# Gated feed-forwards with both terms of a weight tile's upper half in one matmul of 512 columns

## The reference

```python
def conv_glu_ffn(h, w_in, conv_w, conv_b, w_out):
    """Up-projection -> causal depthwise conv (width 3) -> GeGLU -> down-projection."""
    S = h.shape[1]
    u = h @ w_in
    up = jnp.pad(u, ((0, 0), (CONV_WIDTH - 1, 0), (0, 0)))
    u = sum(conv_w[k] * up[:, k:k + S] for k in range(CONV_WIDTH)) + conv_b
    gate, val = jnp.split(u, 2, axis=-1)
    return (jax.nn.gelu(gate, approximate=True) * val) @ w_out
```

## Time and profile before

| | us |
|---|---|
| three runs | 904.54, 904.81, 908.03 (median 904.81) |
| the profiled execution's own time | 907.95 |
| its span, first to last instruction | 906.1 |
| PE busy with matmuls | 849.4 (94%) |
| DVE busy | 620.1 (68%) |
| ACT busy | 469.6 (52%) |
| POOL busy | 134.9 (15%) |
| mean granted TensorE clock | 0.985 of full speed |

### The profile page before, as it was taken

The page is one execution under the profiler, slowest core; times in us unless marked ns, Lnnn a source line. Parts: engine busy times, 40 slices in busy tenths (PEclk is TensorE's granted clock), DMA queues, the critical chain, the costliest instruction groups (busy, mean ns, idle before and its releaser), DMA issues.

```text
span 906.1 us, 15493 instructions
## 1 busy us (share of the span) xinstructions
PE 849.4 (94%) x6073; PEld 788.2 (87%) x6073; DVE 620.1 (68%) x815; ACT 469.6 (52%) x680; POOL 134.9 (15%) x131
## 2 busy tenths in 40 slices
PE   4997998998999999978999999999988799999997
PEld 4997887998899999968999999979776699999996
DVE  6876565669755555696776776877763767767776
ACT  5544667235444444455654554674664465545553
POOL 2261111005100000010112112000221011121110
PEclk9999999999999999999999999999999899999999
DMA  7962233462665555544355455435320444554541
GB/s 287 307 229 94 94 118 115 170 250 93 232 257 185 185 185 186 186 146 157 140 186 203 169 186 205 166 140 187 130 103 1 169 141 167 183 216 158 185 175 47
DMA packets 23064, 152.55 MB, mean 168 GB/s; under 512 B 2443, under 2 KB 3683, under 8 KB 5475
## 3 DMA queue, kind: packets, MB, share of 16 engines
q1 hardware_dynamic: 21648, 145.44, 45.1%
q10 hardware_dynamic: 1363, 6.37, 1.9%
HBM read 150.71 MB, written 1.09 MB: 168 GB/s over the span
## 4 chain that ended last, share of the span: by engine, by line
PE 67%; DVE 6%; ACT 2%; issue 1%; POOL 0%; DVEq 0%; POOLq 0%; ACTq 0%
PE up L974 13%; PE up L976 13%; PE up L975 13%; PE down L980 7%; PE down L981 6%; PE down L982 6%; DVE w_lo L1501 2%; PE up L1010 1%; PE down L1043 1%; PE down L1045 1%; PE down L1180 1%; PE down L1422 1%; PE down L1049 1%; PE up L1446 1%; DVE mid L1767 1%
## 5 line engine op out<-in xcount | busy, mean ns | idle before, releaser
L1501 DVE TENSOR_TENSOR w_lo<-w,w_hi 128x2048 fp32r<-128x2048 f32 x132 | 306.5, 2327 | 77.8 <-ACT w_hi L624 77.6
L974 PE MATMUL up<-x_lo,w_hi 128*128 128x256 f32 x1248 | 357.0, 286 | 1.3 <-DVE w_lo L1501 1.3
L975 PE MATMUL up<-x_hi,w_hi 128*128 128x256 f32 x1248 | 354.1, 284 | 0.0
L976 PE MATMUL up<-x_hi,w_lo 128*128 128x256 f32 x1248 | 354.1, 284 | 0.0
L624 ACT ACTIVATE w_hi<-w 128x2048 fp32r<-128x2048 f32 x132 | 251.6, 1908 | 71.1 <-PE down L982 27.5
L974 PEld LDWEIGHTS up<-x_lo,w_hi 128*128 128x128 f32 x1248 | 240.5, 193 | 3.7 <-DVE w_lo L1501 2.1
L975 PEld LDWEIGHTS up<-x_hi,w_hi 128*128 128x128 f32 x1248 | 240.6, 193 | 1.2
L976 PEld LDWEIGHTS up<-x_hi,w_lo 128*128 128x128 f32 x1248 | 240.4, 193 | 0.0
L980 PE MATMUL down<-w_hi,mid 128*128 128x512 f32 x256 | 100.1, 391 | 0.7 <-DVE w_lo L1501 0.7
L981 PE MATMUL down<-w_hi,mid 128*128 128x512 f32 x256 | 100.0, 391 | 0.0
L982 PE MATMUL down<-w_lo,mid 128*128 128x512 f32 x256 | 99.6, 389 | 0.0
(11 more groups left out here) (243 smaller groups left out, 1049.8 us busy)
## 6 DMA issues: line engine op xcount, KB each, us to landing
w<-w_stream SPq DMA_DIRECT2D x134, 1024.0 KB, 4.8
gates<-vec_store ACTq DMA_DIRECT2D x5, 1024.0 KB, 6.3
region<-rpb SPq DMA_DIRECT2D x2, 768.0 KB, 12.2
gates<-x_in SPq DMA_DIRECT2D x2, 512.0 KB, 4.1
result<-res SPq DMA_DIRECT2D x4, 256.0 KB, 2.0
con<-consts SPq DMA_DIRECT2D x1, 801.0 KB, 6.3
proj<-bands ACTq DMA_DIRECT2D x1, 544.0 KB, 5.2
gates<-vec_store ACTq DMA_DIRECT2D x1, 512.0 KB, 3.8
```

What stands on the lines that cost most here:

```text
L974: m(out_ap, w_hi[slot][:, w_cols:w_cols + P], xl, start=first, stop=False, skip_group_check=True)
L975: m(out_ap, w_hi[slot][:, w_cols:w_cols + P], xh, start=False, stop=False, skip_group_check=True)
L976: return m(out_ap, w_lo[slot][:, w_cols:w_cols + P], xh, start=False, stop=last, skip_group_check=True)
L1501: v.tensor_tensor(lo_of(n), w32[s][:, :], hi_of(n).bitcast(F32), ALU.subtract).then_inc(w_lo_ready, 1)
```

## The change

`x_hi` and `x_lo` become two halves of one tensor `x_both`, so that one matmul can stream both. The up units of the gated feed-forwards go through `glu_unit`: for each weight tile one matmul of `w_hi` with 512 columns (256 of `x_hi`, 256 of `x_lo`) and one of `w_lo` with 256 columns of `x_hi`, which is added to the half that holds the `x_lo` term. A weight tile now fills a whole bank of 512 columns, and a unit two banks. The four banks `up` and `aux` become one tensor `ups`; kind 0 always takes banks 2 and 3, kind 1 banks 0 and 1. Since `aux` is bank 1, the stage's second unit now waits for `rows_ready`. The first unit of a stage keeps its 48 matmuls of 256 columns but also writes the halves apart (`first_glu_unit`).

The two halves have to be added. ACT copies the upper halves of both banks to `probs[kind]` (a buffer that the attention uses elsewhere), 128 x 512; DVE adds them to the lower halves, waits for that result, and then multiplies with the row factors in place. `reads_before` now follows the kind and not the ring slot.

```diff
-        x_hi = [sb(f"x_hi{s}", [P, DC, T], F32R) for s in range(2)]
-        x_lo = [sb(f"x_lo{s}", [P, DC, T], F32R) for s in range(2)]
+        x_both = [sb(f"x_both{s}", [P, 2, DC, T], F32R) for s in range(2)]
+        x_hi = [x_both[s][:, 0, :, :] for s in range(2)]
+        x_lo = [x_both[s][:, 1, :, :] for s in range(2)]
...
-        up = [ctx.enter_context(nc.psum_tensor(f"up{b}", [P, 2 * T], F32)) for b in range(RING)]
-        aux = ctx.enter_context(nc.psum_tensor("aux", [P, 2 * T], F32))
+        ups = ctx.enter_context(nc.psum_tensor("ups", [P, RING + 1, 2 * T], F32))
+        up = [ups[:, b, :] for b in (0, 2, 3)]
+        aux = ups[:, 1, :]
...
+        def glu_bank(kind, t):
+
+            return ups[:, (2, 0)[kind] + t, :]
+
+        def glu_halves(kind):
+
+            both = ups[:, (2, 0)[kind]:(2, 0)[kind] + 2, :]
+            return both[:, :, 0:T], both[:, :, T:2 * T]
...
                 for kind in range(2):
+                    act.wait_ge(unit_done, at.unit(units[kind] + 1))
+                    a.activation(pair_view(probs[kind][:, :]), glu_halves(kind)[1], ACT.Copy).then_inc(low_copied, 1)
                     act.wait_ge(up_read, at.up(UP_INDEX[units[kind]] + 1))
...
+            def glu_unit(at, n, fill, kind):
+
+                s = n % RING
+                pe.wait_ge(w_lo_ready, at.unit(n + 1))
+                if reads_before(n):
+                    pe.wait_ge(up_read, at.up(reads_before(n)))
+                for t in range(2):
+                    bank = glu_bank(kind, t)
+                    for c in range(DC):
+                        w = slice(c * UC + t * P, c * UC + (t + 1) * P)
+                        m(bank, w_hi[s][:, w], x_both[fill % 2][:, :, c, :], start=(c == 0), stop=False,
+                          skip_group_check=True)
+                        ins = m(bank[:, T:2 * T], w_lo[s][:, w], x_hi[fill % 2][:, c, :], start=False, stop=(c == DC - 1),
+                                skip_group_check=True)
+                ins.then_inc(unit_done, 1)
...
-                first_unit(base, fill)
+                first_glu_unit(base, fill)
                 spread(k_pre)
-                unit(STRAIGHT, base + 1, fill)
+                pe.wait_ge(rows_ready, PRE.index(k_pre) + 1)
+                glu_unit(STRAIGHT, base + 1, fill, 1)
...
-                    dve.wait_ge(unit_done, at.unit(n + 1))
-                    v.tensor_tensor(glu_u[kind][:, :, 2:T + 2], pair_view(up[n % RING][:, :]),
+                    dve.wait_ge(low_copied, 2 * at.pair(first + j) + kind + 1)
+                    upper = glu_halves(kind)[0]
+                    chain.link(v.tensor_tensor(glu_u[kind][:, :, 2:T + 2], upper, pair_view(probs[kind][:, :]), ALU.add))
+                    v.tensor_tensor(glu_u[kind][:, :, 2:T + 2], glu_u[kind][:, :, 2:T + 2],
                                     twice(rows[k_pre % 2][:, 0:T]), ALU.mult).then_inc(up_read, 1)
```

More of the change, by code:

```diff
@@ L90, in glu_ups, with glu_kind @@
     return (base + 3 * j - 1, base + 3 * j) if j else (base, base + 1)
+def glu_kind(n):
+    for base in (U_GLU0, U_GLU1):
+        for j in range(PAIRS2):
+            if n in glu_ups(base, j):
+                return base, glu_ups(base, j).index(n)
+    return n % RING
 def output_tile_units():
@@ L106, in reads_before @@
 def reads_before(n):
-    return max([UP_INDEX[m] + 1 for m in UP_INDEX if m < n and m % RING == n % RING], default=0)
+    return max([UP_INDEX[m] + 1 for m in UP_INDEX if m < n and glu_kind(m) == glu_kind(n)], default=0)
 GATES_PAUSE = (1, 8)
@@ L401, in build @@
         conv_first = sem("conv_first")
+        low_copied = sem("low_copied")
         conv_ready = sem("conv_ready")
@@ L1026, in first_unit, with first_glu_unit, term @@
                         ins = term(lo_of(n), x_hi[fill % 2], c, False, True)
+                ins.then_inc(unit_done, 1)
[12 more added lines that the diff above has]
+                                skip_group_check=True)
+                ins.then_inc(unit_done, 1)
+            def first_glu_unit(n, fill):
+                low_last = n in far_hi
+                pe.wait_ge(*((w_hi_ready, n + 1) if low_last else (w_lo_ready, n + 1)))
+                if reads_before(n):
+                    pe.wait_ge(up_read, reads_before(n))
+                def term(w, x, c, half, first, last):
+                    for t in range(2):
+                        ins = m(glu_bank(0, t)[:, half * T:(half + 1) * T], w[:, c * UC + t * P:c * UC + (t + 1) * P],
+                                x[:, c, :], start=(first and c == 0), stop=(last and c == DC - 1), skip_group_check=True)
+                    return ins
+                for c in range(DC):
+                    pe.wait_ge(x_hi_ready, hi_ready(fill, c))
+                    term(hi_of(n), x_hi[fill % 2], c, 0, True, False)
+                    if not low_last:
+                        term(lo_of(n), x_hi[fill % 2], c, 0, False, True)
+                for c in range(DC):
+                    pe.wait_ge(x_ready, DC * fill + c + 1)
+                    ins = term(hi_of(n), x_lo[fill % 2], c, 1, False, True)
+                if low_last:
+                    pe.wait_ge(w_lo_ready, n + 1)
+                    for c in range(DC):
+                        ins = term(lo_of(n), x_hi[fill % 2], c, 0, False, True)
                 ins.then_inc(unit_done, 1)
@@ L1353, in glu @@
                 layer = (U_GLU0, U_GLU1).index(base)
-                first_unit(base, fill)
+                first_glu_unit(base, fill)
                 spread(k_pre)
-                unit(STRAIGHT, base + 1, fill)
+                pe.wait_ge(rows_ready, PRE.index(k_pre) + 1)
+                glu_unit(STRAIGHT, base + 1, fill, 1)
                 def units(at, j):
-                    unit(at, base + 3 * j - 1, fill)
-                    unit(at, base + 3 * j, fill)
+                    glu_unit(at, base + 3 * j - 1, fill, 0)
+                    glu_unit(at, base + 3 * j, fill, 1)
                     pe.wait_ge(mid_ready, PAIRS1 + PAIRS2 * layer + at.pair(j))
@@ L1370, in glu @@
                 for j in (PAIRS2 - 2, PAIRS2 - 1):
-                    for n in glu_ups(base, j):
-                        unit(STRAIGHT, n, fill)
+                    for kind, n in enumerate(glu_ups(base, j)):
+                        glu_unit(STRAIGHT, n, fill, kind)
                 made = PAIRS1 + PAIRS2 * (layer + 1)
@@ L1938, in glu @@
                     at = Looped(i, 4, 2)
-                    chain.enter(i, 4)
+                    chain.enter(i, 8)
                     glu_pair(at, base, layer, 3, k_pre)
```

## The result

The changed kernel took 930.14 us (median of 4 runs, 929.87 to 932.16), the kernel before 905.72 us beside it (median of 4, 904.54 to 908.03). The ratio is 1.0266 with a 95% interval of 1.0242 to 1.0291: slower, by about 24 us. The forecast was 931.1 us. Of all executions two were slow, one of experiment 3 (2199.19 us) and one of the kernel before beside experiments 5, 9 and 10 (1060.43 us); they are in no ratio and no interval, and without them those medians are 919.36 in place of 919.88 and 907.51 in place of 907.53.

What follows compares the result with a forecast made beforehand. PE was taken as the present bound (16.98 us a pair), a DVE-POOL-ACT chain as the new one (17.40). Start, body and tail summed to +14.0 and +12.3, together +26.3 on the median: 931.1 us, range 923 to 937.

Steps and rivals of the forecast that it cites:

- The closed chain: Loop pair: a cycle from DVE's first add through POOL and ACT's last split and copy back to it, 17.40 us.
- Multiply after 0.83: Loop pair, each kind: DVE's add to its multiply, 0.72 us plus 0.11 for the register-valued wait.
- The 0.11 for a wait whose value comes from a register: Extra cost of a DVE wait in the loop, read from taps of 1.90 us inside against 1.79 outside.
- the body: Each stage from pair 1 to pair 9: 138.3 us, +6.9 in layer 0 and +5.2 in layer 1.
- the forecast's rival of a cheaper add: DVE's add in the pairs costs less, without the register's 0.11 or at 0.60 us: 924.7 to 928.5 us; 15%.
- the 9.0 us: Merged matmuls in 42 up units: 0.0133 us per merge, 0.213 a unit, 9.0 us in all if PE stays the bound.
- the first rival: Loop: the new work fits and PE stays the bound, pair of 16.53 us or less, 906 us in all; 3%.
- The start: Each stage up to pair 1: PE's second unit waits for DVE's row-factor copy, +5.1 us per layer.
- 4.4 us of pause: Layer 0's start: PE's second unit waits from 420.14 to the end of DVE's row-factor copy at 424.55.
- a loss of 1.7: Both starts: PE at 1.2 GHz for 3.4 us behind the pause, 1.7 us lost each, bounds 0 and 3.4.
- The tail: Each stage from pair 9 to its end: 35.6 us for 33.6, +2.0 a layer; 26.2 to the last mid_lo.
- the rival of more frequent falls: The clock falls also after PE's pauses in pairs 1 and 10, 1.7 us each, up to four: up to 938; 10%.

Runs made afterwards that it cites:

- experiment 3: Changed kernel with DVE's row-factor copy ahead of the weight split and ACT's down-unit w_hi split behind the next pair's first copy: 919.88 us, ratio 1.0143.
- experiment 5: Changed kernel without ACT's copies and DVE's adds (x_lo term missing), row factors copied first: 906.00 us, ratio 0.9982 to the kernel before.
- experiment 9: experiment 3 with x_hi and x_lo side by side, so the 512 columns are one run: 919.44 us, ratio 1.0131.
- experiment 10: Changed kernel with wider matmuls, copy and add only in pairs 2 to 8, ACT's split moved behind the copy, no row-factor wait: 905.67 us, ratio 0.9972.
- experiment 2: Changed kernel with ACT's w_hi split of the down unit moved behind the next pair's first copy: 926.15 us, ratio 1.0212.
- experiment 6: Kernel before with ACT's copy and DVE's add put in on the whole bank, matmuls and start unchanged: 925.41 us, ratio 1.0205.
- experiment 4: Changed kernel without ACT's copy and DVE's add, so the x_lo term is missing: 913.63 us, ratio 1.0067.
- experiment 7: Kernel before with only the second unit's wait for the row factors added at each stage's start: 917.36 us, ratio 1.0115.
- experiment 8: Changed kernel with 28 unused matmuls of 256 columns filling PE's pause at each stage's start: 928.85 us, ratio 1.0239.
- experiment 1: Changed kernel with DVE's copy of the row factors ahead of a weight split at a stage's start: 926.15 us, ratio 1.0206.

## Why the prediction was right

**The closed chain: right in kind, 0.28 us too long per loop pair.** DVE's add released by ACT's copy and the copy directly behind the last split are what the forecast named, and experiment 2 opens the chain by that one edge: 17.12 becomes 16.79. The term mis-sized is "Multiply after 0.83": it was 0.72 to 0.73 in the loop too. The 0.11 for a wait whose value comes from a register, which the taps show, did not appear between add and multiply, here or in experiment 6. That is 2 x 0.11 of the 0.28. The copy, to its waiter, took 0.61 and not 0.66. Six loop pairs make this 1.7 us a stage, by which the body came out shorter than forecast in layer 1; in layer 0 it is 2.2, the rest from pairs 1 and 2 (16.51 and 16.89 us for 16.96 each). It was the forecast's rival of a cheaper add that held in this term.

**The matmuls: the gain was half of the 9.0 us.** "2 x 0.120 - 0.2267 = 0.0133 us" took the spacing of 512 columns from the down units, where only such matmuls follow each other. Timeline of PE in the changed kernel:

```profile
475.85 0.40 PE L1062 MATMUL ups<-x_both,w_hi 128*128 128x512 f32 x1
476.08 0.28 PE L1064 MATMUL ups<-x_both,w_lo 128*128 128x256 f32 x1
...
476.91 0.40 PE L1062 MATMUL ups<-x_both,w_hi 128*128 128x512 f32 x1
```

Alternating with 256 columns, two matmuls take 0.353 (three times in 1.06), not 0.2267 + 0.120 = 0.347. So a merge saves 0.360 - 0.353 = 0.007 us, a unit 0.11, and 42 units 4.7 us; by the loop pairs, 16.79 for 16.98, it is 0.19 a pair and about 4 us. The Trainium skill (TensorE: Matmul & The Clock Gate, Back-to-back issue gap) would save 0.0025 us by its formula for a matmul alone, an estimated 1.7 us in all; the measured saving lies between this and the forecast. The Trainium skill's figure, in the same section, of about 131 ns for sustained 512-column matmuls does not fit the 0.2267 us of the earlier trace rows. The error cost the forecast nothing, because the chain, and not PE, sets the loop; it cost the first rival, which counted on a pair of 16.53 and 906 us. In experiment 5, where PE is the bound, the stages are 1.8 us shorter and not 9.0.

**The start: right in sum, both parts off in layer 0.** "4.4 us of pause" was 3.35, since the row factors were ready 4.0 us after `spread` began instead of 4.8; "a loss of 1.7" was 3.0 in layer 0 and 1.5 in layer 1. In layer 0 the two nearly cancel, which is luck: +5.7 and +4.8 for +5.1. The mechanism holds. Windows of experiment 2, whose start is the changed kernel's:

```profile
419.33:423.55 4.22, 0.00 (x1) 0.00 (x1) 2.65 (x3) 1.99 (x2) 0.00 (x0) 1.00 0.47 194
424.40:427.80 3.40, 3.40 (x12) 2.91 (x12) 2.20 (x5) 1.10 (x2) 0.00 (x0) 0.50 0.72 289
```

There the pause is 4.2 us, the loss 1.7 and the start +5.3. The length of layer 0's pause goes with the clock ahead of it. Where the clock had fallen during the stage's first unit (before and experiments 2, 4, 6, 7 and 8), the row factors were ready 4.8 us after `spread` began; where it had not (the changed kernel, experiment 10), 4.0. Experiment 1 takes 8.4 us off the two starts by ending the pause. Experiment 8 separates the clock from the wait: 2.5 us in the two stages together.

**The tail: right in layer 0** (from pair 9's first instruction to the last `mid_lo` it is 576.27 to 602.38 = 26.11 us, forecast 26.2), and 1.3 us too short in layer 1. There the last pause of PE cost a clock drop. Window, and timeline of PE behind the pause:

```profile
910.00:915.00 5.00, 3.03 (x9) 2.13 (x8) 3.74 (x4) 0.63 (x1) 0.00 (x0) 0.75 0.00 0
```

```profile
912.45 0.79 PE L1109 MATMUL down<-w_hi,mid 128*128 128x512 f32 x1 [1.97 <-DVE mid L1994]
...
913.47 0.63 PE L1109 MATMUL down<-w_hi,mid 128*128 128x512 f32 x1
913.89 0.63 PE L1111 MATMUL down<-w_hi,mid 128*128 128x512 f32 x1
```

The starts are 0.42 apart where 0.23 is full speed. This is the rival of more frequent falls, which named this place. In layer 0 a pause of 2.0 us at the same place had no such effect. It is no rarity, though: of the 14 tails in the seven profiles with an add in the last pairs (the changed kernel and experiments 1, 2, 3, 6, 8 and 9), all with a pause of 1.92 to 1.97 us, 9 had the fall, and it cost 1.2 to 1.3 us each time. The changed kernel's clock also fell in layer 1 behind pair 1's pause of 1.77 us (0.50 from 758.9 to 762.3); pair 2 took 17.20 us there and 16.90 in layer 0. So 1.7 us each was somewhat high, and a chance of 10% for any extra fall too low.

**Together.** 26.3 was forecast for the stages, 24.1 came. The body's 2.2 and 1.7 and 0.3 of layer 1's start are missing; 0.6 of layer 0's start and the tails' 0.1 and 1.3 go the other way. The medians of the timed runs differ by 24.4. The total is nearer than its parts, by luck: the loop was put too long and the falls of the clock too few; and the increase, 1.9 us too high (26.3 for 24.4), was added to a median of 904.81 where the kernel before took 905.72 beside the changed one, 0.9 more. So 931.1 came within 1.0 of 930.14.

**What stays open.** In this execution the stretch ahead of layer 0's stage was 2.1 us shorter than before. The profile of before has a granted clock of 0.50 from 411.4 to 414.8 us, and the one after has none there. The change touches nothing in that stretch, and the other profiles show that it differs from one execution to the next: `spread` began at 419.8 us before, at 417.6 in experiments 6 and 7, which run the kernel before's code up to there, and at 420.7 and 420.6 in experiments 1 and 4, which run the changed kernel's. The fall named above is not all of it, since experiments 6 and 7 have one too (409.6 to 413.1); what sets the rest is open. Nor do I know why alternating widths cost 0.007 us a pair over the sum of their own spacings. And every sum of stages rests on one profile; those of experiments 1, 5 and 8 are the most touched by where the clock fell.

## What to carry to other kernels

An engine with 30% of idle time can still have no room, if its instructions stand in a fixed order with waits on other engines between them: follow the chain from one period's instruction to the same one of the next, and ask which edge closes it; here one moved instruction on ACT opened it. Price a merge of matmuls by the mix in which they will run, and against what the consumer must now do in addition: here 0.11 us a unit was won, and an add of 0.7, a copy of 0.6 and a wait were paid. And where an old bank gets a new owner, look for the wait that comes with it, since a pause of PE can be paid twice, once in time and once in clock.

## What the runs showed of the hardware

- After a pause of 3.35 us PE was granted 1.2 GHz for 5.9 us of dense matmuls; in experiment 7, after 4.2 us, for some 3.4 us. After 1.97 us at the end of layer 1 the clock fell as well, in layer 0 after 1.96 us it did not; over the seven kernels with an add in the last pairs it fell in 9 of 14 such places. The length of the pause alone did not say what followed.
- A 512-column and a 256-column matmul in turn take 0.353 us, with the 512 columns in one run or in two.
- DVE's dependent add and multiply of 128 x 512 lie 0.72 us apart, in the loop (register-valued wait) and outside it, though the taps do show 1.90 in the loop for 1.79 outside.
